# A hybrid decoder layer on one core: another order of VectorE's sums inside the quads, of the last head's end and of the output's operand sums, and no store of sums at the loop's turn

## The chip, the core and the metric

The kernel runs on one core of a Trainium2 chip. The core has a matrix engine (TensorE, PE in the profile), a vector engine (VectorE, DVE), a scalar engine (ScalarE, ACT) and a GpSimd engine that has next to nothing to do here; SyncE (SP) and ScalarE issue the DMA transfers. The metric is the time of one execution on the device in microseconds, the median of several runs.

## What is computed

One layer over 512 tokens of 2048 channels, in float32. The input projection feeds three branches and the gates:

```python
h = _rmsnorm(x, norm_g[l])
proj = jnp.einsum('bsd,df->bsf', h, w_in[l])
# branch A: differential attention, 8 heads, two softmax maps each
p = p[:, :, 0] - lam * p[:, :, 1]
ya = oa * jax.nn.silu(az)
# branch B: dilated window attention, 3 groups combined by their denominators
yb = ob.reshape(bsz, seq, B_WIDTH) * jax.nn.silu(bz)
# branch C: short gated convolution
yc = cb * conv * jax.nn.silu(cz)
merged = (gates[:, :, 0] * jnp.einsum('bsw,wd->bsd', ya, w_branch_a[l])
          + gates[:, :, 1] * jnp.einsum('bsw,wd->bsd', yb, w_branch_b[l])
          + gates[:, :, 2] * jnp.einsum('bsw,wd->bsd', yc, w_branch_c[l]))
x = x + jnp.einsum('bsd,de->bse', merged, w_out[l])
return _rmsnorm(x, final_g)
```

## The kernel before

**Precision.** A float32 operand is split into a high part (a copy in fp32r, by ScalarE) and a low part (what is left, by VectorE, TENSOR_TENSOR at L1419 in the quads and L1463 in the heads). A product is three matmuls (L587 to L589). So each *unit* of weights, 128 x 1024 words or 512 KB, goes this way: DMA into raw (three buffers) or kb, ScalarE writes w_hi, VectorE writes w_lo, TensorE multiplies. w_hi and w_lo have three buffers each: unit n may be split when TensorE has done unit n - 3 (semaphore pe_used), and a raw buffer is loaded again when its unit is split (lo_done).

**Stages, in order.** Quad 0, plain, 16 units. Quads 1 to 3. Heads 0 to 7, 20 units each, of attention branches A and B with their own projections; heads 1 to 3 and 4 to 6 are the two turns of one hardware loop (pe.Fori(0, 2) and its like on each engine), heads 0 and 7 are written out. Quads 4 to 13, the other projections, with branch C's convolution (the *tail*, eight pieces of 20 units from quad 8 on) in between. Six products of the branches. Two quads of the output.

**A quad** is a product of a 512 x 2048 by a 2048 x 1024 matrix in 2 x 2 blocks, done with seven products in place of eight, 28 units (n = 0 to 27, four for each product p). Its operands are sums of blocks. Sums of weight blocks are made by VectorE in add_units: R1 at units 24 to 27 of the quad before, R3 at 0 to 3, R2 at 4 to 7, R4 at 12 to 15, each a TENSOR_TENSOR on kb. For quads 5 to 13 kb is loaded by SyncE: k2 (2 MB) for the next quad when this quad's last R2 is done, k3 (2 MB) and four of k1 when unit 20 and on are split. Sums of activations are comb_1 to comb_4, of two or three steps each (128 x 2048, VectorE), a high part (comb_high, ScalarE) and a low part (comb_low, VectorE); TensorE waits for comb_lo before the product that needs it. They stand in quad 1, in head 7 and quad 4, and in the output's first quad. Finished products are moved out of PSUM by take_g or take_o at units 2, 6, 10, 14, 18, 22, 26 (two instructions each).

**A head** makes ten blocks of 512 tokens (scale_block; the last two are z_a and z_b), scores, softmax and values. Its branch B lags: scores_b, bias_b (VectorE, writes sc and nmax), exps_b (ScalarE), norm_b (VectorE, writes pr), probs_b (TensorE turns pr), turned_b, values_b, for four classes c = 0 to 3; the end of it lies in the next head, for head 7 in the first units of quad 4. inverse_a is a reciprocal of 128 x 512, norm_o and join_a finish branch A (y_a), low_v and values_b and join_b branch B (y_b).

**Sums of later weights.** During heads 1 to 6 four sums each are made for later stages: ScalarE loads 2 MB into ssum (at unit 0, 5, 10, 15), VectorE does four additions (sum_units, at 2, 7, 12, 17), ScalarE stores 2 MB into s_dram (at 3, 8, 13, 18). 24 in all. In heads 3 and 6 the fourth store is issued at unit 18; behind it come two units and the loop's branch.

Nothing is scheduled by a planner: each engine's order is the program's, and the positions are the numbers in these functions and tables. Every engine works strictly in its order, so an instruction that waits holds up all behind it.

## Time and profile before

| | us |
|---|---|
| median of 3 runs (2548.3 to 2550.77) | 2550.11 |
| the profiled execution | 2549.12 |
| its span, first to last instruction | 2547.3 |
| TensorE busy | 2506.9 |
| VectorE busy | 1961.0 |
| ScalarE busy | 1030.6 |
| mean granted TensorE clock | 0.996 |

The profile is of one execution. Between the span and the time of that execution lie 1.8 us. Three views are used: who waited for whom, by engine; a table of stretches with the number of matmuls in each and the granted clock; and the timeline, one row for each instruction, with the idle time before it in brackets.

### The profile page before, as it was taken

How to read it: one execution, taken by the hardware profiler on the slowest of the kernel's cores; microseconds unless marked ns; L12 is line 12 of the kernel's file. 1: busy time of each engine (PE TensorE's matmuls, PEld its weight loads, DVE VectorE, ACT ScalarE, POOL GpSimd, SP SyncE). 2: the span in 40 equal slices, each digit the busy share in tenths (PEclk: the TensorE clock that was granted, in tenths of full speed). 3: DMA queues.
4: the chain of work that ended last, by engine and by line, in shares of the span. 5: the costliest groups of instructions: out<-in, count | busy, mean ns of one | idle time of the engine just before them, and what ended most of it. 6: DMA issues, size and time to landing. Idle time of an engine off the chain costs nothing.

```text
span 2547.3 us, 30667 instructions
## 1 busy us (share of the span) xinstructions
PE 2506.9 (98%) x11486; PEld 2066.3 (81%) x11486; DVE 1961.0 (77%) x2290; ACT 1030.6 (40%) x1270; POOL 0.2 (0%) x4
## 2 busy tenths in 40 slices
PE   9999999999999999999999999999999999999998
PEld 8878888888888788888887788888878888888786
DVE  8787745768676677777768887788878887898875
ACT  5333333233333233333343433344444445655644
POOL 0000000000000000000000000000000000000000
PEclk9999999999999999999999999999999999999999
DMA  8345243566656566666334645446565456777565
GB/s 319 115 165 188 73 164 97 186 236 219 243 212 250 197 244 213 241 219 236 112 112 157 240 165 190 151 155 205 185 205 198 165 185 222 272 272 248 205 228 195
DMA packets 172421, 501.98 MB, mean 197 GB/s; under 512 B 13553, under 2 KB 50674, under 8 KB 168818
## 3 DMA queue, kind: packets, MB, share of 16 engines
q1 hardware_dynamic: 88160, 338.44, 38.4%
q10 hardware_dynamic: 84114, 161.56, 17.9%
q8 instruction: 94, 1.54, 0.2%
q14 instruction: 53, 0.43, 0.0%
HBM read 407.67 MB, written 92.27 MB: 196 GB/s over the span
## 4 chain that ended last, share of the span: by engine, by line
PE 86%; DVE 7%; DMA 3%; issue 1%; ACT 1%; ACTq 0%; DVEq 0%
PE proj L587 14%; PE proj L589 14%; PE proj L588 14%; PE sc_ps L587 6%; PE sc_ps L589 6%; PE sc_ps L588 6%; PE tr_ps L587 5%; PE tr_ps L589 5%; PE tr_ps L588 5%; PE o_ps L587 3%; PE o_ps L589 3%; PE o_ps L588 3%; DVE w_lo L1419 3%; DMA raw<-s_dram 2%; DMA rows<-c_dram 1%; PE tr_ps L624 1%
## 5 line engine op out<-in xcount | busy, mean ns | idle before, releaser
L587 PE MATMUL proj<-act_hi,w_hi 128*128 128x512 f32 x1280 | 506.5, 396 | 5.7 <-issue 5.7
L589 PE MATMUL proj<-act_hi,w_lo 128*128 128x512 f32 x1280 | 499.8, 390 | 0.0
L588 PE MATMUL proj<-act_lo,w_hi 128*128 128x512 f32 x1280 | 499.3, 390 | 0.0
L937 ACT ACTIVATE w_hi<-raw 128x1024 fp32r<-128x1024 f32 x280 | 296.8, 1060 | 418.2 <-PE proj L589 125.9
L1419 DVE TENSOR_TENSOR w_lo<-raw,w_hi 128x1024 fp32r<-128x1024 f32 x280 | 341.6, 1221 | 156.9 <-ACT w_hi L937 155.8
L937 ACT ACTIVATE w_hi<-kb 128x1024 fp32r<-128x1024 f32 x240 | 254.6, 1061 | 378.0 <-PE proj L589 140.4
L1419 DVE TENSOR_TENSOR w_lo<-kb,w_hi 128x1024 fp32r<-128x1024 f32 x240 | 292.4, 1220 | 105.4 <-ACT w_hi L937 105.2
L1463 DVE TENSOR_TENSOR w_lo<-raw,w_hi 128x1024 fp32r<-128x1024 f32 x160 | 195.8, 1223 | 133.5 <-ACT w_hi L978 130.5
L587 PEld LDWEIGHTS proj<-act_hi,w_hi 128*128 128x128 f32 x1280 | 241.4, 189 | 54.2 <-issue 5.9
L589 PEld LDWEIGHTS proj<-act_hi,w_lo 128*128 128x128 f32 x1280 | 240.8, 188 | 51.3
L588 PEld LDWEIGHTS proj<-act_lo,w_hi 128*128 128x128 f32 x1280 | 241.2, 188 | 48.1
L978 ACT ACTIVATE w_hi<-raw 128x1024 fp32r<-128x1024 f32 x160 | 168.4, 1052 | 227.4 <-PE proj L589 222.4
L1002 ACT ACTIVATE sc<-sc,nmax 128x768 f32<-128x768 f32 (+4 forms) x96 | 65.5, 683 | 230.6 <-DVE nmax L1590 120.3
L587 PE MATMUL sc_ps<-w_hi,act_hi 128*128 128x512 f32 x320 | 126.0, 394 | 4.5 <-DVE w_lo L1419 4.5
L588 PE MATMUL sc_ps<-w_lo,act_hi 128*128 128x512 f32 x320 | 124.6, 389 | 0.0
L587 PE MATMUL tr_ps<-w_hi,act_hi 128*128 128x512 f32 x312 | 121.9, 391 | 2.1 <-DVE w_lo L1419 2.1
L587 PE MATMUL sc_ps<-w_hi,tb 128*128 128x512 f32 x312 | 122.6, 393 | 0.0
L588 PE MATMUL sc_ps<-w_lo,tb 128*128 128x512 f32 x312 | 122.1, 391 | 0.0
L589 PE MATMUL sc_ps<-w_hi,tb 128*128 128x512 f32 x312 | 121.9, 391 | 0.0
L588 PE MATMUL tr_ps<-w_lo,act_hi 128*128 128x512 f32 x312 | 121.4, 389 | 0.0
L589 PE MATMUL sc_ps<-w_hi,act_lo 128*128 128x512 f32 x304 | 118.4, 390 | 0.0
L589 PE MATMUL tr_ps<-w_hi,act_lo 128*128 128x512 f32 x288 | 112.1, 389 | 0.0
(321 smaller groups left out, 4550.0 us busy)
## 6 DMA issues: line engine op xcount, KB each, us to landing
raw<-wst SPq DMA_DIRECT2D x160, 512.0 KB, 4.0
raw<-wg SPq DMA_DIRECT2D x112, 512.0 KB, 4.0
kb<-wg SPq DMA_DIRECT2D x24, 2048.0 KB, 8.2
ssum<-ws ACTq DMA_DIRECT2D x24, 2048.0 KB, 9.1
s_dram<-ssum ACTq DMA_DIRECT2D x24, 2048.0 KB, 7.7
raw<-s_dram SPq DMA_DIRECT2D x96, 512.0 KB, 4.2
raw<-ws SPq DMA_DIRECT2D x72, 512.0 KB, 4.1
kb<-wg SPq DMA_DIRECT2D x48, 512.0 KB, 6.9
```

The costliest lines, as they stand in the source:

```text
L587: nc.tensor.matmul(out, w_h, a_h, start=first, stop=False, skip_group_check=shared)
L588: nc.tensor.matmul(out, w_h, a_l, start=False, stop=False, skip_group_check=shared)
L589: return nc.tensor.matmul(out, w_l, a_h, start=False, stop=last, skip_group_check=shared)
L624: end = nc.tensor.transpose(tr_ps[idx % 2][:, n * P:(n + 1) * P], tile, ident[:, :])
L937: nc.scalar.activation(w_hi[r % RING][:, :], src, ACT.Copy).then_inc(hi_done, 1)
L978: nc.scalar.activation(w_hi[slot][:, :], raw[slot][:, :], ACT.Copy).then_inc(hi_done, 1)
L1002: end = nc.scalar.activation(tile[:, lo:hi], tile[:, lo:hi], ACT.Exp, scale=scale, bias=nmax[:, m:m + 1], accum_out=sums[:, m:m + 1])
L1419: tt(w_lo[r % RING][:, :], src, w_hi[r % RING][:, :].bitcast(f32), ALU.subtract).then_inc(lo_done, 1)
L1463: tt(w_lo[slot][:, :], raw[slot][:, :], w_hi[slot][:, :].bitcast(f32), ALU.subtract).then_inc(lo_done, 1)
```

## The change

1. The times of the sums of weight blocks in a quad become tables: R3 at units 0, 1, 3, 4, R2 at 5, 7, 8, 9, R4 at 12, 13, 15, 16. R1 stays.
2. Quad 1: comb_4's steps go from units 9, 11, 13 to 17, 19, 20, its low part from 18 to 23, its high part on ScalarE from 16 to 21.
3. The sums of later weights: head 0 makes two (at 5 and 10), heads 1 and 2 and their like four, heads 3 and 6 three (0, 5, 10). Still 24.
4. The end of head 7: inverse_a goes ahead of z_b's scale_block. low_v goes from head 7 to unit 4 of quad 4; probs_b 2 and 3 go on TensorE from units 2, 3 to 3, 5, turned_b with them, values_b from unit 5 to 7. norm_o and join_a go from 7 to 12 and 13, join_b from 8 to 9, comb_3 from 9, 10, 11 to 8, 9, 11, comb_4 from 12, 13, 16 to 16, 17, 20, the low parts from 15, 22 to 14, 23. y_a is stored at 15 instead of 9. v_a, v_b and four more tiles change places in memory; the load of k2 in quad 4 no longer waits for y_stored[0], that of k3 does.
5. The output's first quad: g4f's two steps go from unit 12 to 13 and 17, the low parts from 13, 15, 17 to 14, 18, 21, the high parts from 12, 13, 14 to 13, 14, 19.

```diff
-LOAD_AT, SUM_AT, SAVE_AT = [{at + n: n // 5 for n in (0, 5, 10, 15)} for at in (0, 2, 3)]
+LOAD_AT, SUM_AT, SAVE_AT = 0, 2, 3
+SUMS_AT = {0: (5, 10), 1: (0, 5, 10, 15), 2: (0, 5, 10, 15), 3: (0, 5, 10), HEADS - 1: ()}
+SUMS_BEFORE = {0: 0, 1: 2, 2: 6, 3: 10, HEADS - 1: 0}
+SUMS_LOOP = 11
+ADD_3, ADD_2, ADD_4 = (0, 1, 3, 4), (5, 7, 8, 9), (12, 13, 15, 16)
...
                 if n == 16:
                     sp.wait_ge(o_free, 2 * HEADS + 1)
-                    sp.wait_ge(y_stored[0], 16 * (HEADS + 1))
                     load_k2(QUADS_V + 1)
                 if n == 19:
+                    sp.wait_ge(y_stored[0], 16 * (HEADS + 1))
                     load_k3(QUADS_V + 1)
...
-                        if 1 <= n < 4:
-                            probs_b(HEADS - 1, n)
-                        if n == 5:
+                        if n in (1, 3, 5):
+                            probs_b(HEADS - 1, (n + 1) // 2)
+                        if n == 7:
                             values_b(HEADS - 1)
...
                     if last and w == 9:
                         turned_b(i, 0)
                         bias_b(i, 1)
+                        inverse_a(i)
                     scale_block(h, w)
...
                             norm_b(i, 1)
                             bias_b(i, 2)
-                            inverse_a(i)
-                            low_v(2 * i + 2, v_b)
...
-                if n < 4:
-                    add_units(R3, q, n)
-                if 4 <= n < 8:
-                    add_units(R2, q, n - 4)
-                if 12 <= n < 16:
-                    add_units(R4, q, n - 12)
+                for kind, at in ((R3, ADD_3), (R2, ADD_2), (R4, ADD_4)):
+                    if n in at:
+                        add_units(kind, q, at.index(n))
...
-                        if n in (9, 11, 13):
-                            comb_4((n - 9) // 2)
+                        if n in (17, 19, 20):
+                            comb_4((17, 19, 20).index(n))
...
-                    if q == 0 and n == 12:
+                    if q == 0 and n == 13:
                         dve.wait_ge(comb_sum, 11)
                         link(tt(g4f, g3f, m11, ALU.add))
+                    if q == 0 and n == 17:
                         tt(g4f, g4f, m21, ALU.subtract).then_inc(comb_sum, 1)
```

Three places in the order of instructions. First VectorE in quad 1 from unit 9 on, before (w_lo is a unit's split, tb_f a step of comb_4, `kb<-kb,raw` an R4, gin an eviction, rstd the row of roots):

```order
L1419 TENSOR_TENSOR w_lo1<-kb,w_hi1 128x1024
L1546 SCALAR_TENSOR_TENSOR tb_f<-tb,act_hi 128x2048
L1419 TENSOR_TENSOR w_lo2<-kb,w_hi2 128x1024
L1761 TENSOR_SCALAR gin<-o_ps,nrcol 128x512
L1761 TENSOR_SCALAR gin<-proj0,nrcol 128x512
L1419 TENSOR_TENSOR w_lo0<-kb,w_hi0 128x1024
L1548 TENSOR_TENSOR tb_f<-tb_f,tb 128x2048
L1419 TENSOR_TENSOR w_lo1<-raw1,w_hi1 128x1024
L1445 TENSOR_TENSOR kb<-kb,raw1 128x1024
L1513 COPY rstd<-proj1 128x512
L1419 TENSOR_TENSOR w_lo2<-raw2,w_hi2 128x1024
L1445 TENSOR_TENSOR kb<-kb,raw2 128x1024
```

and now:

```order
L1427 TENSOR_TENSOR w_lo1<-kb,w_hi1 128x1024
L1450 TENSOR_TENSOR kb<-kb 128x1024
L1427 TENSOR_TENSOR w_lo2<-kb,w_hi2 128x1024
L1771 TENSOR_SCALAR gin<-o_ps,nrcol 128x512
L1771 TENSOR_SCALAR gin<-proj0,nrcol 128x512
L1427 TENSOR_TENSOR w_lo0<-kb,w_hi0 128x1024
L1427 TENSOR_TENSOR w_lo1<-raw1,w_hi1 128x1024
L1453 TENSOR_TENSOR kb<-kb,raw1 128x1024
L1521 COPY rstd<-proj1 128x512
L1427 TENSOR_TENSOR w_lo2<-raw2,w_hi2 128x1024
L1453 TENSOR_TENSOR kb<-kb,raw2 128x1024
L1427 TENSOR_TENSOR w_lo0<-raw0,w_hi0 128x1024
```

The steps on tb_f are gone from here (they stand behind the splits of units 17, 19 and 20); the last R2 has moved in, to unit 9.

VectorE at the end of head 7, before. z_b is the last block's scaling, `rsum<-sums` and pr are norm_b, the rows from `sc<-masks` to nmax bias_b, tmp_a the reciprocal of inverse_a:

```order
L1576 TENSOR_TENSOR z_b<-proj1,rstd 128x512
L1419 TENSOR_TENSOR w_lo1<-raw1,w_hi1 128x1024
L1617 RECIPROCAL rsum<-sums 128x1
L1618 TENSOR_SCALAR pr<-sc,rsum 128x768
L1606 SCALAR_TENSOR_TENSOR sc<-masks,slope,sc_ps0 128x512
L1608 SCALAR_TENSOR_TENSOR sc<-masks,slope,sc_ps1 128x128 x2
L1612 TENSOR_REDUCE rsum<-sc 128x1
L1613 TENSOR_SCALAR nmax<-rsum 128x1
L1661 RECIPROCAL tmp_a<-tmp_a 128x512
L1657 TENSOR_TENSOR v_lo<-v_b,v_hi 128x512
L1419 TENSOR_TENSOR w_lo2<-raw2,w_hi2 128x1024
```

and now:

```order
L1621 TENSOR_SCALAR nmax<-rsum 128x1
L1669 RECIPROCAL tmp_a<-tmp_a 128x512
L1584 TENSOR_TENSOR z_b<-proj1,rstd 128x512
L1427 TENSOR_TENSOR w_lo1<-raw1,w_hi1 128x1024
L1625 RECIPROCAL rsum<-sums 128x1
L1626 TENSOR_SCALAR pr<-sc,rsum 128x768
L1614 SCALAR_TENSOR_TENSOR sc<-masks,slope,sc_ps0 128x512
L1616 SCALAR_TENSOR_TENSOR sc<-masks,slope,sc_ps1 128x128 x2
L1620 TENSOR_REDUCE rsum<-sc 128x1
L1621 TENSOR_SCALAR nmax<-rsum 128x1
L1427 TENSOR_TENSOR w_lo2<-raw2,w_hi2 128x1024
```

The reciprocal stands ahead of z_b and of the next unit's split, and v_lo is gone from in front of the third split.

ScalarE at the end of the loop's body, from the last head's exponentials (`sc,sums<-sc,nmax`) to the branch, before:

```order
L1002 ACTIVATE sc,sums<-sc,nmax 128x768
L977 REGISTER_ALU
L978 ACTIVATE w_hi1<-raw1 128x1024
L1063 DMA s_dram<-ssum 128x4x1024
L977 REGISTER_ALU
L978 ACTIVATE w_hi2<-raw2 128x1024
L1009 REGISTER_ALU
```

and now:

```order
L1012 ACTIVATE sc,sums<-sc,nmax 128x768
L987 REGISTER_ALU
L988 ACTIVATE w_hi1<-raw1 128x1024
L987 REGISTER_ALU
L988 ACTIVATE w_hi2<-raw2 128x1024
L1019 REGISTER_ALU
```

The 2 MB store of ssum is no longer there.

## Rows read from the trace of the kernel before

**Rows 1.** The page: an engine's busy time, one costly group (ns of one)

```profile
PE 2506.9 (98%) x11486; PEld 2066.3 (81%) x11486; DVE 1961.0 (77%) x2290; ACT 1030.6 (40%) x1270; POOL 0.2 (0%) x4
...
L937 ACT ACTIVATE w_hi<-raw 128x1024 fp32r<-128x1024 f32 x280 | 296.8, 1060 | 418.2 <-PE proj L589 125.9
```

**Rows 2.** Who waited for whom, TensorE: us, times, longest us

```profile
PE proj L587 <- issue: 5.7, 1, 5.7
PE tr_ps L587 <- DVE w_lo L1419: 4.8, 5, 2.1
...
PE tr_ps L624 <- DVE pr L1618: 3.9, 3, 2.2
```

**Rows 3.** Stretches, TensorE: stretch, its us, busy us (matmuls), clock, DMA, GB/s

```profile
106.00:150.00 44.00, 41.37 (x180) 1.00 0.35 120
150.00:194.00 44.00, 44.00 (x196) 1.00 0.53 192
...
1384.00:1428.00 44.00, 39.36 (x164) 1.00 0.82 308
...
1890.00:1920.00 30.00, 28.16 (x121) 1.00 0.47 152
2066.00:2084.00 18.00, 17.81 (x79) 1.00 0.30 103
2411.00:2447.00 36.00, 33.28 (x143) 1.00 0.65 224
```

**Rows 4.** Timeline, TensorE, loop's turn: start, us, what [idle before]

```profile
828.07 0.71 PE L624 MATMUL tr_ps<-ident,pr 128*128 128x128 f32 x5
834.47 0.79 PE L587 MATMUL proj<-act_hi,w_hi 128*128 128x512 f32 x1 [5.68 <-issue]
```

**Rows 5.** Timeline, VectorE's first row after its own turn

```profile
836.24 0.15 DVE L1681 COPY slope<-slopes 128x1 f32 x1 [2.67 <-issue]
```

**Rows 6.** DMA queues in 824.6 to 831.7 us: packets, MB, share of 16 engines

```profile
q10 hardware_dynamic: 526, 2.10, 84.1%
q1 hardware_dynamic: 21, 0.09, 2.9%
```

**Rows 7.** The same in 831.7 to 833.0 us

```profile
q8 instruction: 1, 0.02, 4.2%
```

**Rows 8.** Stretches, all engines: stretch, us, busy of each, clock, DMA, GB/s

```profile
832.40:839.20 6.80, 4.74 (x11) 3.77 (x12) 2.08 (x7) 2.07 (x4) 0.00 (x0) 0.50 0.28 110
...
1361.40:1364.90 3.50, 3.50 (x11) 2.73 (x10) 3.25 (x6) 1.54 (x2) 0.00 (x0) 0.51 0.45 150
```

**Rows 9.** Timeline, VectorE in quad 1: start, us, what

```profile
98.77 1.23 DVE L1419 TENSOR_TENSOR w_lo<-kb,w_hi 128x1024 fp32r<-128x1024 f32 x1 [3.08 <-ACT w_hi L937]
...
103.50 1.40 DVE L1817 TENSOR_SCALAR gin<-proj,rcol 128x512 f32<-128x512 f32 x2
...
110.42 1.22 DVE L1419 TENSOR_TENSOR w_lo<-kb,w_hi 128x1024 fp32r<-128x1024 f32 x1
...
136.40 2.28 DVE L1550 TENSOR_TENSOR tb_f<-tb_f,act_lo 128x2048 f32<-128x2048 f32 x1
```

**Rows 10.** Timeline, TensorE: two transposes in quad 4

```profile
1354.90 0.87 PE L624 MATMUL tr_ps<-ident,pr 128*128 128x128 f32 x6 [1.39 <-DVE pr L1618]
...
1360.77 0.44 PE L624 MATMUL tr_ps<-ident,pr 128*128 128x128 f32 x2 [2.23 <-DVE pr L1618]
```

**Rows 11.** Timeline, VectorE around the last head's end

```profile
1342.42 0.69 DVE L1576 TENSOR_TENSOR z_b<-proj,rstd 128x512 f32<-128x512 f32 x1 [1.42 <-PE proj L589]
...
1347.99 3.34 DVE L1661 RECIPROCAL tmp_a<-tmp_a 128x512 f32<-128x512 f32 x1
...
1357.31 1.22 DVE L1419 TENSOR_TENSOR w_lo<-raw,w_hi 128x1024 fp32r<-128x1024 f32 x1
```

**Rows 12.** Who waited for whom, 1386 to 1424 us, all engines

```profile
ACT w_hi L937 <- DMA raw<-s_dram: 18.6, 7, 6.5
```

**Rows 13.** The source line of kb's first load, all 12 of them

```profile
DMA to landing us min/median/max: 7.7/8.1/9.2
```

More of the change, by code:

```diff
@@ L104, in bank, with sums @@
         return (NBLK1 * self.k + w) % RING
+    def sums(self, t, at):
+        if t - at not in SUMS_AT[self.k]:
+            return None
+        m = SUMS_BEFORE[self.k] + SUMS_AT[self.k].index(t - at)
+        return m if self.j is None else SUMS_LOOP * self.j + m
     def loads(self, t):
@@ L234, in program @@
             s1("pad1", [P, 512 - 4 * 64 - 2 * 64 - 8])
+            v_a, v_b = s1("v_a", [P, 4, P]), s1("v_b", [P, 4, P])
+            z_a, th = s1("z_a", [P, T]), s1("th", [P, T])
+            y_b, z_b = s1("y_b", [P, T]), s1("z_b", [P, T])
             pr = s1("pr", [P, 6 * P])
             s1("pad4", [P, 2 * P])
-            z_a, th = s1("z_a", [P, T]), s1("th", [P, T])
-            y_b, z_b = s1("y_b", [P, T]), s1("z_b", [P, T])
-            v_a, v_b = s1("v_a", [P, 4, P]), s1("v_b", [P, 4, P])
             s1("pad2", [P, 16])
@@ L1052, in split @@
                         split_1(h, t)
-                    if last or fresh:
-                        return
-                    if t in LOAD_AT:
-                        m = 4 * i + (LOAD_AT[t] - 4)
-                        if h.j is not None:
-                            act.wait_ge(osum_stored, 16 * m + 16)
+                    m = h.sums(t, LOAD_AT)
+                    if m is not None:
+                        act.wait_ge(osum_stored, 16 * m + 16)
                         act.dma_start(ssum[:, :, :], ws[bass.ds(m, 1), :, :, :].rearrange("o t p q -> p (o t) q")).then_inc(osum_in, 16)
-                    if t in SAVE_AT:
-                        m = 4 * i + (SAVE_AT[t] - 4)
+                    m = h.sums(t, SAVE_AT)
+                    if m is not None:
                         act.wait_ge(osum_done, m + 1)
@@ L1195, in _ @@
                         comb_high(3, t3[0], f3, (comb_sum, 3))
-                    if q == 1 and n == 16:
+                    if q == 1 and n == 21:
                         comb_high(4, t4[0], f4, (comb_sum, 4))
@@ L1677, in split @@
                         split_1(h, t)
-                    if t in SUM_AT and not last and not fresh:
-                        sum_units(4 * i + (SUM_AT[t] - 4))
+                    m = h.sums(t, SUM_AT)
+                    if m is not None:
+                        sum_units(m)
                 link(nc.vector.tensor_copy(slope[:, 0:1], slopes[:, bass.ds(4 * i, 1)]))
@@ L1750, in take_g @@
                     dve.wait_ge(brow_in, 16 * (q - QUADS_C + 1))
+                if q == QUADS_V and p == 2:
+                    dve.wait_ge(y_ready, HEADS)
                 if q == QUADS_V and p == PRODUCTS - 1:
@@ L1888, in _ @@
             head(fixed(0))
-            links = steps["n"] - before + 8 + 8
+            links = 3 * (steps["n"] - before - 2 * len(SUMS_AT[0]) + 8) + 2 * SUMS_LOOP
             with dve.Fori(0, 2) as j:
-                enter(j, 3 * links)
+                enter(j, links)
                 for k in range(1, 4):
@@ L1912, in _ @@
                         if n == 4:
+                            low_v(2 * HEADS, v_b)
+                        if n == 5:
                             turned_b(HEADS - 1, 2)
                             norm_b(HEADS - 1, 3)
-                        if n == 5:
+                        if n == 7:
                             turned_b(HEADS - 1, 3)
-                        if n == 7:
-                            norm_o(HEADS - 1)
-                            join_a(HEADS - 1)
                         if n == 8:
                             silu(HEADS - 1, 1, BZ)
+                        if n == 9:
                             join_b(HEADS - 1)
-                        if n in (9, 10, 11):
-                            comb_3(n - 9)
-                        if n in (12, 13, 16):
-                            comb_4((12, 13, 16).index(n))
-                        if n == 15:
+                        if n in (8, 9, 11):
+                            comb_3((8, 9, 11).index(n))
+                        if n == 12:
+                            norm_o(HEADS - 1)
+                        if n == 13:
+                            join_a(HEADS - 1)
+                        if n in (16, 17, 20):
+                            comb_4((16, 17, 20).index(n))
+                        if n == 14:
                             comb_low(t3[1], f3, t3[0], 7)
-                        if n == 22:
+                        if n == 23:
                             comb_low(t4[1], f4, t4[0], 8)
```

25 lines of the change are left out of this document (13 added, 12 removed).

## The prediction

> **What bounds the kernel now.** First the engines' totals: TensorE is busy for 2506.9 of 2547.3 us [rows 1], so the work itself can't move and only the 40 us in which TensorE stands still can. Then the view of who waited for whom, TensorE alone: 5.7 us are one single wait that the profile calls "issue", 4.8 us are waits for VectorE's w_lo in front of tr_ps alone, 3.9 us are waits of transposes for pr [rows 2]. These are lower bounds, since a matmul's end is modelled and covers part of a wait. The better measure is a count: an undisturbed stretch of 44 us in a quad holds 196 matmuls, 0.2245 us each [rows 3]; a disturbed stretch of the same length holds fewer, and the missing ones times 0.2245 are what it lost (small transposes have to be taken off by hand).
>
> What VectorE is to a quad: a unit is 12 matmuls, 12 x 0.2245 = 2.7 us. Of the three weight buffers the one for unit n is free when TensorE has done unit n - 3; then ScalarE takes 1.06 us [rows 1] and VectorE 1.22 us (1.14 from start to start when it has a queue) [rows 9]. An undisturbed w_lo is thus ready about 2 x 2.7 - 1.06 - 1.22 = 3.1 us before it is needed. VectorE may be late by some 2.8 us and costs nothing; beyond that each 0.1 us is TensorE's. So what counts is how VectorE's extra work is bunched, not its sum.
>
> **The change part by part. The loop's turn.** TensorE's last transposes before the branch start at 828.07, its next matmul at 834.47, 5.68 us idle [rows 4]. VectorE's own turn, later, costs it 2.67 us [rows 5]. The difference is visible in the DMA queues: from 824.6 to 831.7 the ScalarE queue moves the 2 MB store of the sums (84% of 16 engines), and no instruction queue has a packet; the first one is in 831.7 to 833.0 [rows 6, 7]. I take that TensorE's fetch stood behind the store. The change moves head 3's last sum out: no store in flight there, and 4 sums (4 x 1.2 us of VectorE) less just before. The gap then should be that of VectorE, plus 0.6 for a fetch of 16 KB where VectorE's is 8 KB (0.02 and 0.01 MB in the rows): an estimate of 3.3 us, gain 2.4, between 0 (the store was innocent) and 3.0 (the gap becomes 2.67). After the gap the granted clock is 0.5 (1.2 GHz) from 832.4 to 839.2, TensorE works 4.74 us in it, so 2.4 us are lost [rows 8]. After the smaller gap of 2.23 us in the last head it was at 0.51 for 3.5 us, 1.7 lost [rows 8, 10]. I take 1.7 for the new gap too: gain 0.7 (0 to 2.4). **Turn: 3.1 us, 0 to 5.4.** DMA: Bandwidth & Descriptors in the Trainium skill (section "Queues, rings and completion order") says that a DMA engine takes turns between its queues at every packet; by that a fetch would wait for one packet, whatever the store's size, and the gain here would be near 0. The trace speaks against a fair turn: loads of raw issued in the same stretch moved 0.09 MB while the store moved 2.10 [rows 6].
>
> **Quad 1.** From 106 to 150 us TensorE does 180 matmuls, 4 of them small ones that row_of_roots needs, against 196: 20 x 0.2245 = 4.5 us lost [rows 3]. VectorE is one unbroken queue there: 1.14 for each split, 1.13 for each sum, 2.2 for each step of comb_3, comb_4 and their low parts [rows 9]. The change takes 3 x 2.2 us (comb_4) from units 9, 11, 13 to 17, 19, 20, the low part from 18 to 23, a sum out of units 2, 6 and 14, which also evict (1.32). Summing again from the split of unit 2 (ends 100.0 [rows 9]): unit 5's split ends 110.7 instead of 111.6 and TensorE starts it at 111.2 without a wait; unit 9's at 122.0 is on the edge (0.3 us); from unit 10 on VectorE is 1 to 3 us ahead. At 17 to 20 the three steps of 2.2 make it late by 1.6 us at most, and there the full 3 us of lead stand. ScalarE's high part (1.9 us) at 21 makes one w_hi 2 us late: covered too. R4's later places delay only loads that unit 24 needs. **4.3 us, 3 to 4.6.**
>
> **End of the last head, quad 4.** TensorE waits for pr of 7's turns at 1354.9 (1.39) and 1360.8 (2.23) [rows 10], with starts 1.55 and 2.4 behind; clock 1.7 [rows 8]; some 0.4 more before. 6.1 us in all. The chain is VectorE's: z_b 1342.4, ..., the reciprocal of 3.34 us at 1348.0, then split of unit 3 only at 1352.0, norm, bias, split of unit 4 at 1357.3 [rows 11]. The change moves the reciprocal ahead of z_b. This is not free: bias_b(1) ends at 1341.0, z_b can start at 1344.35 instead of 1342.4, and TensorE's unit 0 needs z_b's bank, so it starts at 1345.2, not 1343.3: **a new wait of 1.9 us**. Behind it: unit 3's split ends 1352.8, turns of class 1 are read by 1354.1, norm_b(2) 1355.0, bias_b(3) 1357.4, unit 4's split 1358.55. Since TensorE now turns class 2 after unit 3 (at 1357.8, pr is there) it wants unit 4 at 1358.4 and waits 0.5. Class 3 comes after unit 5, values after unit 7, both without a wait. Of 6.1 us 2.4 remain: **3.7 us, 1.5 to 4** (a clock at half after the 1.9 us wait would cost 1.7; other gaps of that size left it at full).
>
> **Rest of quad 4.** 1384 to 1428 holds 164 matmuls against 196, 7.2 us lost [rows 3]. Two causes in one: VectorE's six steps of 2.2 us at units 9 to 16, and DMA: ScalarE waits 18.6 us for raw<-s_dram there [rows 12], since a unit is loaded only when VectorE is done with the one three before, and four big loads of kb go by. The change spreads the steps over 8, 9, 11, 16, 17, 20 and puts norm and join at 12 and 13. By the same summing no unit up to 20 is late (the smallest lead left is 0.45 us, unit 18). New on VectorE is a wait of 1.2 us: join_b stands at unit 9, and the values that it reads come after unit 7 (which ends at 1358.9 + 4 x 2.7 + 0.6 of transposes = 1370.4) and take 3.2 us as before (16 small and 12 large matmuls), to 1373.7; behind it stand comb_3's second step and unit 10, needed at 1379.1, ready 1377.7. The queue of SP: kb's first load no longer waits for y_stored of head A's, the second one does. At unit 21 the load (8 us in this crowd) remains the bound: 2.6 us wait; 0.6 more at 22 to 24. **4.0 us, 1.5 to 6.5.**
>
> **Quads 5 to 13.** Per unit the order is smoother (the sum leaves units 2, 6, 14). Most quads have no wait to lose. 1890 to 1920 holds 121 where 134 fit, 2.8 us, 0.5 of it transposes [rows 3]: the tail's loads come late and units 25 to 3 catch up. Only unit 3's share (0.9) goes, since 0 and 1 keep their sums. Around 2066 to 2084 a lateness of 0.5 goes. **1.4 us, 0.5 to 2.5.**
>
> **The output's first quad.** 2411 to 2447 holds 143 against 161: 4.0 us [rows 3], half of it one wait of 2.1 for unit 13 (the longest in front of tr_ps [rows 2]). It goes: its split then ends at 2413.0, needed 2415.5. But comb_low 13 now stands with an eviction before unit 15 (0.4 us), comb_low 14 with one before unit 19 (1.0), and unit 22 still waits for its load, issued when unit 19 is split, behind 1 MB of x (1.6). **0.8 us, -0.5 to 3.**
>
> **Sum.** 3.1 + 4.3 + 3.7 + 4.0 + 1.4 + 0.8 = 17.3 us. The profiled execution took 2549.1 us (span 2547.3), 1.0 under the median of 2550.1; median after: 2550.1 - 17.3 = 2532.8.
>
> **Rivals.** (1) *The turn keeps its gap* (the store is innocent, by the rule cited): 14.2 us, 2535.9. Chance 0.15. (2) *DMA is the wall of quads 4 and of the output*: TensorE, no longer held by VectorE, meets loads that come no sooner; the three terms 4.0, 0.8 and 1.4 go to nothing: 11.1 us, 2539.0. For it: 18.6 us of waits for loads [rows 12]. Against: a load is issued by VectorE's progress, which is earlier. 0.17. (3) *Slower*: kb's load for the next quad is issued after the last R2, now at unit 9 instead of 7, 5.4 us later, in ten quads. It takes 7.7 to 9.2 us [rows 13]; the next load on SP's queue, raw for unit 15, follows the sum of unit 12, 3 units (8.2 us) behind: room for the median of 8.1 by a hair. Raw can come 0.5 + 2.8 us late before TensorE waits; to cost more than the 17.3 + 5 us in ten quads it would have to be 3.3 + 2.3 = 5.6 us late in each. Only with loads of over 13 us; 0.03: about 2556. (4) *The change is without effect*, since missing matmuls are missing records and not waits: 0.03, 2549. The forecast has 0.62.
>
> The lowest ends (0 + 3 + 1.5 + 1.5 + 0.5 - 0.5 = 6) and the highest (26) are not met all at once; 8 in 10 is 9 to 24: **2526 to 2541**. A measurement can tell 0.2% (5 us) from no change: faster 0.93, same 0.04, slower 0.03.
>
> **What would show it.** TensorE's "issue" wait near 3.3 and no store in the 4 us before it; the 44 us from 106 on with 190 matmuls or more; a new wait of proj for z_b about 7 us earlier than 1343, and no 2.23 us wait of a transpose; ScalarE still waiting over 10 us for raw<-s_dram in quad 4; near 10 us of TensorE waits in all where 29 are. Wrong would be: an issue wait of 5 or more, waits in quads 5 to 7, where none are now (kb's load), or a clock at half in quad 4.

## The result

| | before | after |
|---|---|---|
| median of the runs (us) | 2549.97 (2548.3 to 2550.77, 4 runs) | 2534.22 (2533.49 to 2535.23, 4 runs) |
| the profiled execution | 2549.12 | 2534.20 |
| its span | 2547.3 | 2532.4 |
| mean granted TensorE clock | 0.996 | 0.997 |

The changed kernel takes 0.9935 of the time (95% interval 0.9922 to 0.9948). The forecast was 2532.8, range 2526 to 2541. The median is 1.4 us off the forecast; the terms of the sum are further off than that, in both directions.

The engines' totals of the page after, with TensorE's 2506.9 of [rows 1] to be put beside them. TensorE's idle time fell by 9.7 us and its busy time by 5.2: half clock took 3.4 us here (two times 1.7) where it took 4.1, and a modelled end in front of each wait counts as busy, so fewer waits are probably less of that too.

```profile
span 2532.4 us, 30658 instructions
PE 2501.7 (99%) x11486; PEld 2067.4 (82%) x11486; DVE 1964.4 (78%) x2290; ACT 1031.7 (41%) x1270; POOL 0.2 (0%) x4
```

Who waited for whom, TensorE, after: total, number of times, longest. Compare [rows 2].

```profile
PE tr_ps L597 <- DVE w_lo L1427: 6.0, 6, 2.1
PE proj L597 <- DVE w_lo L1427: 2.1, 1, 2.1
PE o_ps L597 <- DVE w_lo L1427: 2.1, 2, 1.2
...
PE proj L597 <- issue: 1.7, 1, 1.7
PE proj L597 <- DVE z_b L1584: 1.6, 1, 1.6
...
PE tr_ps L634 <- DVE pr L1607: 0.8, 1, 0.8
PE tr_ps L634 <- DVE pr L1626: 0.3, 1, 0.3
```

The issue wait is 1.7 where it was 5.7, and the transposes' waits for pr of the last head are 0.3 where they were 3.9. Two entries are new, z_b (forecast) and pr at L1607, and the one wait of proj for w_lo grew from 0.9 to 2.1. All waits of this view together are 19.5 us where they were 28.9.

Stretches of the kernel after: length, busy time and count of TensorE, of its weight loads, VectorE, ScalarE and GpSimd, granted clock, DMA share, GB/s. The four are quad 1, the units of quad 4 that [rows 3] has at 1384, a piece of quad 13, and the output's first quad.

```profile
106.00:150.00 44.00, 43.78 (x198) 36.03 (x197) 42.40 (x38) 18.51 (x17) 0.00 (x0) 1.00 0.37 125
1369.00:1413.00 44.00, 41.92 (x177) 34.00 (x177) 36.87 (x31) 18.41 (x17) 0.00 (x0) 0.96 0.92 339
2087.00:2099.00 12.00, 9.91 (x46) 7.84 (x45) 7.33 (x8) 6.04 (x7) 0.00 (x0) 1.00 0.49 158
2396.00:2432.00 36.00, 35.79 (x158) 29.19 (x157) 33.95 (x28) 21.42 (x25) 0.00 (x0) 1.00 0.68 236
```

Quad 1 went from 180 matmuls to 198 and is all but undisturbed. The piece of quad 4 went from 164 to 177, not to 196, with its clock below 1. The output's quad went from 143 to 158 of 161. Quad 13 loses 2 us in 12 where the kernel before lost nothing.

**Where the 14.9 us came from.** Taken from the two traces as the difference between the ends of the same units on TensorE (a minus is a gain). Of quad 1's 4.1 us, 0.14 stand already at the end of the first unit of all. The last row adds the values before rounding.

| place | forecast | measured |
|---|---|---|
| quad 1 | -4.3 | -4.1 |
| head 0 | 0 | +0.8 |
| the loop's turn | -3.1 | -6.2 |
| last head's end (up to unit 8 of quad 4) | -3.7 | -3.7 |
| rest of quad 4 | -4.0 | -3.1 |
| quads 5 to 13 | -1.4 | +3.8 |
| products of the branches | 0 | +0.7 |
| output | -0.8 | -3.2 |
| sum | -17.3 | -14.9 |

The rows behind the four that differ most. TensorE at the turn:

```profile
827.21 0.49 PE L597 MATMUL proj<-act_hi,w_hi 128*128 128x512 f32 x1 [1.68 <-issue]
```

TensorE at unit 17 of quad 4; a stretch right behind it; and ScalarE, which splits that unit, and the load it waits for (DMA view of 1377 to 1378.5: KB each, us from issue to landing):

```profile
1390.78 0.50 PE L597 MATMUL proj<-w_hi,act_hi 128*128 128x512 f32 x1 [2.08 <-DVE w_lo L1427]
```

```profile
1392.00:1395.20 3.20, 3.20 (x9) 2.46 (x9) 3.17 (x4) 0.00 (x0) 0.00 (x0) 0.50 0.93 394
```

```profile
1388.33 1.06 ACT L947 ACTIVATE w_hi<-raw 128x1024 fp32r<-128x1024 f32 x1 [6.63 <-DMA raw<-s_dram]
```

```profile
raw<-s_dram SPq DMA_DIRECT2D x1, 512.0 KB, 10.5
y_dram<-y_a ACTq DMA_DIRECT2D x1, 256.0 KB, 9.6
```

Quad 13, unit 17: SyncE's issues, ScalarE, VectorE and TensorE. The last load of y (kb<-y_dram) is issued at 2086.45, behind the load of raw at 2086.08 in SyncE's queue; ScalarE and VectorE both stand until it has landed, and TensorE's next w_lo is behind them.

```profile
2086.08 0.33 SPq L410 DMA_DIRECT2D raw<-wg  x1
2086.45 0.44 SPq L509 DMA_DIRECT2D kb<-y_dram  x1
```

```profile
2092.29 1.06 ACT L1229 ACTIVATE tb<-kb 128x1024 fp32r<-128x1024 f32 x1 [6.25 <-DMA kb<-y_dram]
```

```profile
2092.29 1.23 DVE L1783 TENSOR_TENSOR tb_f<-kb 128x1024 f32<-128x1024 f32 x1 [3.86 <-DMA kb<-y_dram]
```

```profile
2095.61 0.50 PE L597 MATMUL tr_ps<-w_hi,act_hi 128*128 128x512 f32 x1 [2.08 <-DVE w_lo L1427]
```

### The profile page after: what moved, and what is told of

Read it like the earlier page. It is cut to its first block, busy times and chain, and to the rows that moved or that the text cites. A ratio compares the mean times of both kernels' runs of the same rounds, so it can differ in the third digit from the quotient of the medians.

```text
span 2532.4 us, 30658 instructions
## 1 busy us (share of the span) xinstructions
PE 2501.7 (99%) x11486; PEld 2067.4 (82%) x11486; DVE 1964.4 (78%) x2290; ACT 1031.7 (41%) x1270; POOL 0.2 (0%) x4
## 4 chain that ended last, share of the span: by engine, by line
PE 90%; DVE 4%; DMA 3%; ACT 1%; issue 1%; ACTq 0%; DVEq 0%; SPq 0%
PE proj L597 15%; PE proj L599 15%; PE proj L598 15%; PE sc_ps L597 6%; PE sc_ps L599 6%; PE sc_ps L598 6%; PE tr_ps L597 5%; PE tr_ps L598 5%; PE tr_ps L599 5%; PE o_ps L599 3%; PE o_ps L598 3%; PE o_ps L597 3%; DVE w_lo L1427 2%; DMA rows<-c_dram 1%; PE tr_ps L634 1%; DMA raw<-s_dram 1%
```

## Experiments

Each run's gain or loss at a place is read like the table above, from the ends of units in its trace. Executions of one kernel differ by up to 5.6 us (the first kernel below), partly by the clock (last section) and partly by how long loads take, so short effects are read at their place and not from the total. The times, with the kernel before as measured beside each:

| kernel | us, median | runs | before | ratio, 95% interval |
|---|---|---|---|---|
| old distribution of the sums | 2535.93 (2534.69 to 2540.26) | 4 | 2549.30 | 0.9945, 0.9930 to 0.9961 |
| before, 32 KB store | 2542.01 (2541.18 to 2545.37) | 7 | 2549.30 | 0.9973, 0.9962 to 0.9985 |
| before, 1 MB store | 2543.69 | 1 | 2549.30 | |
| all sums' places old | 2533.32 (2531.76 to 2535.38) | 5 | 2549.30 | 0.9940, 0.9926 to 0.9953 |
| R4's places old | 2528.64 | 1 | 2550.01 | |
| reciprocal old | 2536.18 | 1 | 2550.01 | |
| reciprocal late | 2534.71 | 1 | 2550.01 | |
| k2 early | 2534.71 (2532.30 to 2535.81) | 4 | 2550.01 | 0.9940, 0.9923 to 0.9957 |
| k2 and k3 in pieces | 2532.20 | 1 | 2552.25 | |
| head 0's sums late | 2535.00 | 1 | 2552.25 | |
| g4f old | 2539.27 | 1 | 2551.92 | |
| both new waits taken out | 2529.13 (2527.92 to 2532.30) | 5 | 2551.92 | 0.9913, 0.9899 to 0.9926 |

### Is it the store that held the turn?

Three kernels. The first is the changed one with the old distribution of the sums:

```diff
-SUMS_AT = {0: (5, 10), 1: (0, 5, 10, 15), 2: (0, 5, 10, 15), 3: (0, 5, 10), HEADS - 1: ()}
-SUMS_BEFORE = {0: 0, 1: 2, 2: 6, 3: 10, HEADS - 1: 0}
-SUMS_LOOP = 11
+SUMS_AT = {0: (), 1: (0, 5, 10, 15), 2: (0, 5, 10, 15), 3: (0, 5, 10, 15), HEADS - 1: ()}
+SUMS_BEFORE = {0: 0, 1: 0, 2: 4, 3: 8, HEADS - 1: 0}
+SUMS_LOOP = 12
```

> The changed kernel with the old distribution of the sums of later weights: none in head 0, four each in heads 1 to 6, so the fourth store of heads 3 and 6 is again issued at unit 18, ahead of the loop's branch. Theory (the 2 MB store in flight is what held the turn): TensorE's issue wait at 830 us goes from 1.7 back to 5.7, the clock is at half for some 7 us behind it, and the turn costs 6.2 us more; head 0's wait for pr (0.8) goes; in all +5.4 us against the changed kernel, about 2539.6. Rival (the turn became cheaper for another reason, such as the addresses of four tiles or the length of the loop's code): issue stays at 1.7, no half clock, and only the 0.8 of head 0 is gained: about 2533.4.

Measured at the turn: as the theory has it.

```profile
830.38 0.79 PE L597 MATMUL proj<-act_hi,w_hi 128*128 128x512 f32 x1 [5.71 <-issue]
```

```profile
828.60:835.40 6.80, 5.02 (x12) 3.96 (x13) 1.81 (x5) 2.04 (x4) 0.00 (x0) 0.50 0.25 96
```

The turn costs 6.4 us more than in the changed kernel, the wait in head 0 is gone (-0.8). The profiled execution took 2540.26 (expected 2539.6), but that is partly chance: it also lost and gained some us in quads 4, 9 and 13. The median of the four runs is 1.7 above the changed kernel's and not 5.4. The interval, applied to the 2549.30 of before, reaches from 2531.5 to 2539.4: the rival's 2533.4 lies in it and the theory's 2539.6 just above. So the totals do not confirm the size, and what the turn cost in the three runs of 2534.69 to 2536.36 is not known. The theory rests on this one trace and on the next two kernels.

The other two are the kernel before, whose fourth store of heads 3 and 6 is cut down, while VectorE's additions and all semaphores stay. They leave out the rest of two sums. Not shown below: two transfers of 2 MB in head 0 that fill those sums' place, and ScalarE's wait for them in front of the small store.

```diff
-                        act.dma_start(s_dram[bass.ds(m, 1), :, :, :].rearrange("o t p q -> p (o t) q"), ssum[:, :, :]).then_inc(osum_stored, 16)
+                        part = (1, 64) if h.k == 3 and t == 18 else (4, HU)
+                        act.dma_start(s_dram[bass.ds(m, 1), 0:part[0], :, 0:part[1]].rearrange("o t p q -> p (o t) q"),
+                                      ssum[:, 0:part[0], 0:part[1]]).then_inc(osum_stored, 16)
```

> The kernel before, but the fourth store of heads 3 and 6 writes 32 KB (64 of 1024 columns of one block) in place of 2 MB. VectorE's four additions, ScalarE's order and all waits stay. The rest of these two sums is left out (their place in memory is filled in head 0 with unsummed weights, by two transfers of 2 MB from memory to memory). Theory (bytes in flight delay TensorE's fetch at the branch): issue near 1.7 to 2, no half clock, 5 to 6.2 us gained against before at the turn, 2544 to 2545. Rival (VectorE's four additions of 4.8 us, or ScalarE's wait for them, make the turn long): issue stays at 5.7 with the clock at half, 2550.

> As the one with the small store, but 1 MB of the 2 MB is stored at unit 18 of heads 3 and 6 (two of four blocks; the others are left out). If the gap is the wait for the store's end, it shrinks by the time of the missing bytes: the full store ran from about 824.6 to 831.7, so 1 MB is done 3 to 3.5 us earlier, which leaves an issue wait of 2 to 2.5 us. If the gap depends on whether any large transfer is there (fetch behind a queue's prefetched descriptors), it stays above 4. If additions on VectorE are the cause, 5.7.

With 32 KB and with 1 MB (here part is (2, HU)), TensorE's first matmul behind the turn:

```profile
830.19 0.49 PE L588 MATMUL proj<-act_hi,w_hi 128*128 128x512 f32 x1 [1.55 <-DVE w_lo L1471]
```

```profile
831.73 0.49 PE L588 MATMUL proj<-act_hi,w_hi 128*128 128x512 f32 x1 [2.38 <-DVE w_lo L1471]
```

6.4 us are gained at the turn with the small store, 5.5 with the half one; the clock stays at 1.00. The small store's totals agree: 7.3 us between the medians of 12 and 7 runs, where 5 to 6.2 were expected. So the bytes are the cause, and VectorE's 4.9 us of additions are not: they stand in both. What is left with the small store is named as a wait for w_lo, since these additions make that split late: it ends at 830.16, TensorE starts at 830.19. With 1 MB the same split (the row below) ends at 830.87 and TensorE starts only at 831.73, so there the label is wrong and it was still the fetch.

```profile
829.65 1.22 DVE L1471 TENSOR_TENSOR w_lo<-raw,w_hi 128x1024 fp32r<-128x1024 f32 x1
```

The times line up by the store's end. The DMA view gives it (issue and us to landing), here for the kernel with the old distribution and for 1 MB:

```profile
s_dram<-ssum ACTq DMA_DIRECT2D x1, 2048.0 KB, 7.6
```

```profile
s_dram<-ssum ACTq DMA_DIRECT2D x1, 1024.0 KB, 4.1
```

Issued at 820.64 it landed at 828.25, and TensorE went on at 830.38; 1 MB issued at 825.30 landed at 829.39, TensorE at 831.73; in the kernel before, 824.68 and 7.66, so 832.34, and TensorE at 834.47 [rows 4]. That is 2.13, 2.34 and 2.13 us behind the store's end, each time. With no large store TensorE's step over the turn, from the last transposes to the next matmul, is 1.15 to 1.95 us (eleven traces), where it is 5.96 and 5.98 with 2 MB and 2.65 with 1 MB.

The packets show the fetch itself. TensorE resumes 2.6 to 3.2 us after the start of a 16 KB packet on its instruction queue (q8), in all fourteen traces. Without a large store that packet starts 0.9 to 1.5 us ahead of the last transpose. With one it starts when the store's last packet ends: at 831.79 and 831.80 in the kernel before, 827.70 and 827.75 with the old distribution, 829.04 and 829.04 with 1 MB. The DMA view of the last, 826.2 to 829.0 and then 829.0 to 829.1:

```profile
q10 hardware_dynamic: 271, 1.05, 94.7%
```

```profile
q8 instruction: 1, 0.02, 54.9%
q10 hardware_dynamic: 1, 0.00, 0.4%
```

### The sums' places in the quads

```diff
-ADD_3, ADD_2, ADD_4 = (0, 1, 3, 4), (5, 7, 8, 9), (12, 13, 15, 16)
+ADD_3, ADD_2, ADD_4 = (0, 1, 2, 3), (4, 5, 6, 7), (12, 13, 14, 15)
```

> The changed kernel with the old places of the sums of weight blocks (R3 at units 0 to 3, R2 at 4 to 7, R4 at 12 to 15) in all quads. Theory: quad 13's waits at units 17 and 19 (2.4 and 0.4 us, loads of branch B's y queued on SyncE behind the load that waits for R4 of unit 2) go; the lateness at quad 11 unit 3 (0.9) and quad 13 unit 7 (0.5) comes back; in quad 1 up to 1 us of the gain is lost again near units 5 to 9. Net between -2 and +0.5 us against the changed kernel, 2532.2 to 2534.7. Rival (the tables are what gains in quad 1, not the later steps of comb_4): quad 1 loses 2 us or more of its 4.1, and the net is slower by 0.7 us or more.

The same with R4's places alone, (12, 13, 14, 15):

> The changed kernel with R4 back at units 12 to 15 in all quads, R3 and R2 in the new places. Theory (SyncE's load that waits for R4 of unit 2 holds the load of y behind it in quad 13): the waits at units 17 and 19 of quad 13 (2.4 and 0.4 us) go, 2.8 us gained there, quad 1 and units 3 and 7 of quads 11 and 13 unchanged within 0.3. Rival (the later R2, which holds the first y loads, is the cause): the step at unit 17 stays at 2 us or more.

All places old: quad 1 loses 0.9 of its 3.9 (units 5 to 9; the traces differ by another 0.2 before the first unit), quad 11 unit 3 and quad 13 unit 7 lose 0.9 and 0.5, quad 13's units 17 and 19 give 2.4 and 0.4. The theory's four numbers all came; the rival's 2 us in quad 1 did not, so 3.0 of quad 1's 3.9 are comb_4's and the low part's. The median is as the changed kernel's. R4 alone old: the 2.4 and 0.4 in quad 13 go as well, and quad 1 and units 3 and 7 of quads 11 and 13 stay. The rest of what this one execution is faster by (0.8 at the turn, 1.7 at quad 4's unit 17, 2.3 at quad 9's unit 23) varies as much between traces of the same code. ScalarE waits for that load for 2.75 us where it was 6.25, and TensorE does not wait at all from 2080 to 2100:

```profile
2086.04 1.06 ACT L1229 ACTIVATE tb<-kb 128x1024 fp32r<-128x1024 f32 x1 [2.75 <-DMA kb<-y_dram]
```

So R4's later units are what costs these 2.8 us. In the eight traces that have them, unit 17 of quad 13 loses 2.0 to 5.4 us, with the half clock where one follows; in the six without them, the kernel before included, it loses nothing. The loss comes through SyncE's order (the load of raw that waits for R4 of unit 2, now at unit 15, stands ahead of the load of y), and R2's later units are innocent.

### Where the reciprocal stands

```diff
                         bias_b(i, 1)
-                        inverse_a(i)
...
                             bias_b(i, 2)
+                            inverse_a(i)
```

> The changed kernel with the reciprocal (inverse_a, 3.34 us) back behind bias_b of class 2, where it was before, all else as changed. Theory (the reciprocal's place at z_b costs 1.9 us, and VectorE has a hole of 2.05 us behind bias_b(2) that it can use): TensorE's wait for z_b at unit 0 of quad 4 (step 1.90) goes, unit 4's excess of 0.75 stays; 1.9 us gained up to unit 7 against the changed kernel. Rival (what my prediction assumed: behind bias_b(2) it is the 3.34 us that made the transposes late): waits for pr of 1.4 and 2.2 us return, 2 us or more lost.

Or at unit 7 of quad 4, behind turned_b(HEADS - 1, 3):

> The changed kernel with the reciprocal at unit 7 of quad 4, behind the last turns. Theory: no wait for z_b (1.9 gained) and none at unit 4 (0.75 gained), so 2.65 earlier at unit 7; then VectorE is 3.3 us later, of which its wait for o_ps takes 1.5; unit 10 (lead 1.35) and unit 12 (lead 1.00) give back 0.5 to 1.0; in all -1.7 to -2.2 at unit 16. Rival (DMA, not VectorE, sets units 8 to 16): the 2.65 are lost to units 13 to 17, whose loads come no sooner: 0.

The wait for z_b goes in both, -1.89 at unit 0, what the changed kernel's step of 1.90 says. In the first, unit 4 takes 1.33 back, since the reciprocal now stands between bias_b(2) and the split:

```profile
1338.63 3.35 DVE L1669 RECIPROCAL tmp_a<-tmp_a 128x512 f32<-128x512 f32 x1
1342.01 1.23 DVE L1427 TENSOR_TENSOR w_lo<-raw,w_hi 128x1024 fp32r<-128x1024 f32 x1
```

It is between the theory (1.9 gained up to unit 7) and the rival (2 or more lost), 0.6 gained: the reciprocal ahead of z_b costs 1.9 us, and its new place is worth 1.3; by itself it is a loss of 0.5 us, and the gain at the last head's end (3.7, so 4.2 without this loss) is made by the other edits there. Which of them (the later turns, the later low_v, the later y_a) was not tried apart.

With the reciprocal at unit 7 the kernel is 1.8 us ahead at unit 7, where 2.65 were expected: unit 4's wait did not go. Units 10 and 12 give back 1.1, so 0.5 are left at unit 16 (expected 1.7 to 2.2), and at unit 24 it is 0.7 *behind*. Neither the theory nor the rival gave these numbers. Which leads to the next question.

### Quad 4: is it VectorE or the transfers?

```diff
-                if n == 16:
+                if n == 12:
                     sp.wait_ge(o_free, 2 * HEADS + 1)
                     load_k2(QUADS_V + 1)
```

> The changed kernel with quad 4's load of k2 (2 MB) behind the load of unit 12 instead of 16 in SyncE's order, so issued near 1365 instead of 1376.4, where the 16 DMA engines are busy to 0.37 and 0.52. Theory (unit 17's load took 10.5 us because it was issued 1.4 us behind 2 MB of kb): it lands in 5 to 7 us, unit 17's step of 2.47 goes, and with it the half clock behind it, 2.5 to 4.2 us less than the changed kernel up to unit 24: 2530 to 2532. Rival (bandwidth is short over the whole of units 12 to 24, so the wait only moves): a wait of 2 us or more at units 13 to 16 or at 18 to 21, gain under 1 us.

And k2 and k3 in eight loads of 512 KB, issued behind the loads of units 12, 13, 14, 16, 18 (two) and 19 (two), where the changed kernel has one load of 2 MB at 16 and one at 19:

> The changed kernel with quad 4's two loads of 2 MB (k2, k3) cut into eight of 512 KB, issued behind the raw loads of units 12, 13, 14, 16, 18 (two) and 19 (two). Theory (quad 4 is short of bandwidth from 1376 to 1410 only, the engines stand at 0.37 to 0.52 before; and 2 MB in one piece puts 10 us on the raw load behind it): no load over 8 us, waits at units 13 to 24 in all under 1.5 us where the changed kernel loses 2.77 at unit 17 with the half clock; 1.5 to 3 us gained at unit 24. Rival (VectorE's comb steps, not bytes, set units 13 to 20): waits at 15 and 20 of 1.5 to 2 us each as when k2 alone came early, gain under 1 us.

Time on TensorE from the end of unit 18 of head 7 to the end of quad 4's units, us, worked out from the traces:

| kernel | to unit 7 | to unit 16 | to unit 17 | to unit 20 | to unit 24 |
|---|---|---|---|---|---|
| before | 42.8 | 69.9 | 73.8 | 82.7 | 96.3 |
| after | 35.9 | 63.6 | 70.3 | 78.5 | 89.5 |
| after, another execution (R4 old) | 35.9 | 63.6 | 68.4 | 77.3 | 89.2 |
| reciprocal old | 35.3 | 63.0 | 69.5 | 79.2 | 91.6 |
| reciprocal late | 34.1 | 63.1 | 68.1 | 77.9 | 90.2 |
| k2 early | 35.9 | 65.8 | 68.6 | 78.8 | 90.9 |
| k2 and k3 in pieces | 35.9 | 63.6 | 66.3 | 77.0 | 89.2 |

Seven traces have quad 4 exactly as changed (the two above, the old distribution, all places old, head 0 late, g4f old, both waits out). They end unit 17 at 68.0 to 70.3 and unit 24 at 89.2 to 91.3, so differences of 2 us at unit 24 tell nothing. The changed kernel's own trace is the worst of them at unit 17: the half clock followed there in none of the other six.

Whatever is gained up to unit 17, nothing of it is left at unit 24: all kernels but the one before are within 89.2 and 91.6. Unit 17's wait went with k2 early and with the pieces, as the theory said, and came back at units 15 and 20 to 22, or 19 to 22, so both theories' totals (2530 to 2532, and 1.5 to 3 us gained) missed. The rivals had the size right, under 1 us. But the second one put the waits down to VectorE's comb steps, and at units 19 and 20 VectorE itself stands idle, behind ScalarE, which waits for the load. Unit 20 with the pieces:

```profile
1395.90 1.06 ACT L952 ACTIVATE w_hi<-raw 128x1024 fp32r<-128x1024 f32 x1 [3.11 <-DMA raw<-s_dram]
```

```profile
1397.00 1.23 DVE L1432 TENSOR_TENSOR w_lo<-raw,w_hi 128x1024 fp32r<-128x1024 f32 x1 [2.95 <-ACT w_hi L952]
```

With k2 early ScalarE waits 6.09 us for unit 20's load and VectorE 3.95 us for ScalarE. VectorE has its share at unit 15 with k2 early, where a low part and two evictions stand ahead of the split and the queue was late from a load that ScalarE had waited 4.55 us for, and at unit 21, 0.6 us behind the third comb step. So most of what came back are waits for transfers. 1376 to 1410 of the kernel after, and the same stretch with the pieces:

```profile
1376.00:1410.00 34.00, 31.92 (x135) 25.91 (x134) 26.90 (x23) 12.72 (x12) 0.00 (x0) 0.95 0.99 377
```

```profile
1376.00:1410.00 34.00, 31.86 (x137) 24.93 (x135) 27.39 (x22) 13.13 (x12) 0.00 (x0) 1.00 0.91 334
```

The 16 DMA engines are busy to 0.99. With the pieces 1.5 MB have gone ahead, but k3 waits for y_a's store (y_stored[0]), and that, in the same crowd, takes 7.5 us and lands at 1384.7:

```profile
y_dram<-y_a ACTq DMA_DIRECT2D x1, 256.0 KB, 7.5
```

With the pieces the DMA engines are at 0.91 and the result is no better, so bytes alone may not be all of it. A load is also issued only when VectorE has split the unit three before; how much that adds was not tried.

### Head 0, and the entry of the loop

```diff
-SUMS_AT = {0: (5, 10), 1: (0, 5, 10, 15), 2: (0, 5, 10, 15), 3: (0, 5, 10), HEADS - 1: ()}
+SUMS_AT = {0: (10, 15), 1: (0, 5, 10, 15), 2: (0, 5, 10, 15), 3: (0, 5, 10), HEADS - 1: ()}
```

> The changed kernel with head 0's two sums of later weights loaded at units 10 and 15 instead of 5 and 10. Theory (four additions of 1.22 us at unit 7 stand ahead of a bias and a norm whose result TensorE turns at 383.7): the step of 1.08 there goes, 0.8 us gained up to head 1. Rival (a store in flight at unit 18 also hurts where the loop is entered, not only where it turns back): a wait of 2 us or more at head 0's last units, with the clock perhaps at half. At the later turn nothing changes (1.6 to 2.0).

The step at 384 us and with it 0.82 us are gone, and head 0's last units and the loop's first are unchanged, although a store of 2 MB is now issued at unit 18 there too. The store was issued at 442.43 and took 7.4 us, over the entry. What the store held is thus found at the jump back alone, in this trace and in that of the last kernel below. This is the row of the changed kernel which is no longer a wait:

```profile
384.80 0.44 PE L634 MATMUL tr_ps<-ident,pr 128*128 128x128 f32 x2 [0.75 <-DVE pr L1607]
```

### The output's first quad

```diff
-                    if q == 0 and n == 13:
+                    if q == 0 and n == 12:
                         dve.wait_ge(comb_sum, 11)
                         link(tt(g4f, g3f, m11, ALU.add))
-                    if q == 0 and n == 17:
                         tt(g4f, g4f, m21, ALU.subtract).then_inc(comb_sum, 1)
```

> The changed kernel with both steps of g4f back at unit 12 of the output's first quad (one is at 13, one at 17 now), all else as changed. Theory (the two steps of 2.2 us bunched between the splits of units 12 and 13 made the longest wait of the kernel before there): unit 12's split ends 2400.3, two steps and a split later it is 2405.9 against a need of 2403.8, so a new step at unit 13 of 2.1 to 2.4 us more than a unit's 2.72, and 0.2 less at unit 15: +2 us at unit 24 against the changed kernel, 1.7 more if the clock falls to half. Rival (the loads of x and raw, which came in 5.6 and 4.5 us here and in 9.6 and 7.5 in the kernel before, are what was gained): under 0.5 us.

Unit 13 takes 4.05 us more, unit 15 0.53 less. 2.33 of the 4.05 are the wait, the rest is the clock, at half for 3.4 us right behind it:

```profile
2403.41 2.29 DVE L2095 TENSOR_TENSOR tb_f<-tb_f,act_hi_f 128x2048 f32<-128x2048 f32 x1
2405.62 2.35 DVE L1427 TENSOR_TENSOR w_lo<-raw,w_hi 128x1024 fp32r<-128x1024 f32 x2
```

```profile
2407.00:2410.30 3.30, 3.30 (x8) 2.65 (x9) 3.30 (x3) 0.00 (x0) 0.00 (x0) 0.50 0.73 216
```

At unit 24 it is 4.1 us behind, by the differences within the quad. The theory holds (2 us and the half clock, 3.7), the rival (x's loads) does not.

### Both new waits taken out

> The changed kernel with R4 back at units 12 to 15 and head 0's sums at 10 and 15. Theory: the two waits that the change made new and that single edits removed (2.8 us in quad 13, 0.8 in head 0) go, all else stays: a median of 2530.6 (2534.2 less 3.6), ratio to the kernel before 0.992; the clock at half for 3.4 us after none, one or two waits of 2 us, which is chance and moves a run by 1.7 us each. Rival (what is gained in quad 13 is lost in the loads behind it, or the single run of 2528.6 with R4 back was luck with the clock alone): 2533 to 2535, as the changed kernel.

R4 is back at units 12 to 15 and head 0's sums are at 10 and 15. 2529.13 us, median of 5, where 2530.6 was expected: 0.9913 (0.9899 to 0.9926) of the kernel before, where 0.992 was expected. The changed kernel's own ratio is 0.9935 (0.9922 to 0.9948). The two intervals overlap a little, so the step between the two is likely, not certain, by the totals; at its places it is there: -2.4 and -0.4 in quad 13, -0.8 in head 0. The rest of this trace's lead of 4.5 us over the changed kernel's is 2.0 us each at unit 17 of quad 4 and unit 23 of quad 9, mostly their half clocks, less what other places give back. The stretch in quad 13 that had 46 matmuls has 54:

```profile
2087.00:2099.00 12.00, 12.00 (x54) 9.91 (x54) 11.18 (x12) 9.69 (x11) 0.00 (x0) 1.00 0.27 96
```

In its profiled execution no gap was followed by a half clock, which in the changed kernel's cost 2 x 1.7 us.

## Why the prediction was right, and where it was not

**The turn: right cause, size wrong.** The forecast named the store and the experiments confirm it, 32 KB against 2 MB alone. It gave 3.1 us and it was 6.2, 4.0 of the gap and 2.2 of the clock. Two terms failed. The gap was taken as VectorE's 2.67 plus 0.6 for a longer fetch, 3.3; it is 1.7. VectorE's gap was no lower bound for TensorE's, and there was no row for the added 0.6 but a ratio of bytes. And a half clock of 1.7 us was carried over from the 2.23 us gap of [rows 8, 10]; none came, there or in any trace without the full store. The first range (0 to 5.4) did not hold 6.2, since its end used the same 2.67.

**Rival 1, the store is innocent,** fell. The trace had spoken against it beforehand [rows 6], and the three store sizes settle it: TensorE resumes 2.1 to 2.3 us behind the store's end. Loads were held back as the fetch was: while the store ran they got 0.09 MB beside its 2.10 in the kernel before [rows 6], and with the old distribution 0.12 beside 1.10 (824 to 827.75). DMA: Bandwidth & Descriptors in the Trainium skill ("Queues, rings and completion order") has a DMA engine take turns between its queues at every packet, a packet being some 9 to 17 descriptors and at most 64. The prediction took a packet for something short and concluded that the size of the store would not matter. That does not follow. The trace has the 2 MB as 512 pieces of 4 KB, 32 for each of 16 engines. If a piece is one descriptor, an engine's share is two or three packets of the typical size, or a single one; with a single one the rule allows what was seen. Which it is, no run here shows.

**Quad 1: 4.3 forecast, 4.1 measured.** The unit by unit sum of VectorE's queue held, down to unit 9 being the edge (0.3 forecast, 0.5 measured). Without the 0.14 from before the first unit it is 3.9.

**The last head's end: 3.7 and 3.7.** The new wait for z_b was forecast as 1.9 us and is 1.9; unit 4's as 0.5 and is 0.75. The order on VectorE, its ScalarE and TensorE could be summed, because no transfer is involved. This is the place where a cost of the change, not only its gain, was read from the trace before.

**Rest of quad 4: 4.0 and 3.1, by the wrong reasoning.** VectorE's summing was right up to unit 16 (no wait there). The step that failed is "no unit up to 20 is late" and, behind it, "At unit 21 the load (8 us in this crowd) remains the bound: 2.6 us wait". Unit 21 lost nothing; unit 17 lost 3.7, 2.0 of wait and 1.7 of clock. Its load had taken 7.4 us before. It took 10.5, issued 1.4 us behind the 2 MB of kb and beside y_a's store, which was moved to unit 15; in the six other traces with this quad it took 9.8 to 10.2. That both are the cause is argued: with k2 early or in pieces the load took less and its wait went, and y_a's store was not moved alone. Rival 2 (transfers are the wall) was given 0.17 for all of quad 4, the tail and the output together, at 2539.0. Its mechanism is what the rows show in quad 4 from unit 17 on; its price, all of the 4.0 lost, did not come, and for the output it is not true.

**Quads 5 to 13: -1.4 forecast, +3.8 measured.** The gains came (0.9 at quad 11's unit 3, 0.5 in quad 13). What failed is a step that is missing: of R4's move from 14 and 15 to 15 and 16 the forecast says, for quad 1, that it delays only loads that unit 24 needs. True there; in quad 13 the loads of y stand behind them. The rest, 1.9 and 0.7 us, is at quads 9 and 12, where the tail waits for rows<-c_dram. These steps vary by over 1 us between traces of the same code, and a half clock followed the first of them here.

**Head 0: forecast 0, measured +0.8.** The sums moved there were counted as free without a look at what stands behind the four additions.

**Output: -0.8 and -3.2.** Unit 13's 2.1 us wait went as forecast (2.4), unit 15's came (0.5 for 0.4). Units 19 and 22 were to wait 1.0 and 1.6; they waited 0.05 and not at all. x's load and raw's landed in 5.6 and 4.5 us, where the one before had 9.6 and 7.5 and the forecast kept those. Here the transfer times were taken too long, in quad 4 too short. Unit 22 waited in none of the eleven traces of changed kernels; unit 19 waited 0.05 to 0.95, so the 1.0 forecast for it was not far off for another execution.

**The signs.** No store stood before the turn, the 44 us from 106 on held 198 matmuls, z_b's wait came and the 2.23 us wait went, and ScalarE still waited 14.9 us for raw<-s_dram in quad 4, all as named. TensorE's waits in all were to be near 10 us and are 19.5. Of the three signs of being wrong one came, the half clock in quad 4; an issue wait of 5 and waits in quads 5 to 7 did not.

**The total was luck.** It came out within 1.4 us (2.4 in the traces) because the turn and the output were underrated by 5.5 us and what had been left at nothing or overrated (head 0, quads 4 to 13, the branches) made it 7.6 worse. The two terms that were right within 10%, quad 1 and the last head's end, are those with no transfer in them.

## What to carry to other kernels

A large store in flight when TensorE jumped back in this loop delayed its instructions until 2.1 to 2.3 us behind the store's end: keep the last units before a branch free of large transfers, or at least finish them earlier. When a unit of work is moved by one step, follow each semaphore that it raises to the queue that waits for it, in each place where the same table is used, to the last quad: the one exception in the code (loads of y instead of kb) was the one that cost. Where the DMA engines are busy to 0.99, as here in quad 4, a load's duration before the change was no estimate for after, and gains upstream were given back; count the bytes and the share first.
